# Whole gate or up matrices as buffer units in a decoder layer's expert stage, and a second entry buffer

## The chip, the core and the metric

The kernel runs on one core of one Trainium2 chip. The metric is the device time of one execution in microseconds (us), as the median of several runs. Five engines with queues of their own work side by side: TensorE (PE, matrix products; its weight loads are shown as PEld), VectorE (DVE), ScalarE (ACT), GpSimd (POOL) and SyncE (SP), which here issues all loads of weights. Sixteen DMA engines carry the bytes out of the chip's main memory. Order between engines is kept by semaphores that the kernel counts by hand.

## The reference

One decoder layer over 256 tokens of width 2048, float32. The change touches its last block only, the mixture of experts: 32 experts of inner width 256 in 4 groups; each token goes to two experts of one group.

```python
combine = jnp.sum(jax.nn.one_hot(flat, N_EXPERTS) * wts[..., None], axis=1)   # two weights per token
for grp in range(N_GROUPS):
    sl = slice(grp * EXPERTS_PER_GROUP, (grp + 1) * EXPERTS_PER_GROUP)
    hid = (jax.nn.silu(jnp.einsum("nd,edf->nef", hf, w_gate[sl]))
           * jnp.einsum("nd,edf->nef", hf, w_up[sl]))
    y = y + jnp.einsum("nef,efd->nd", hid * combine[:, sl, None], w_down[sl])
x = x + y;  out = rmsnorm(x, lnf_g)
```

Each expert has three matrices of 2 MiB: gate and up (2048 x 256), down (256 x 2048).

## The kernel before, in words

Experts are worked on in 16 pairs (`NPAIR`). Tokens are first sorted by expert with products against one-hot matrices (`gather`, line 1554), which fill `hs`, all entries by expert in 16 chunks of 128 model columns. For each pair the entries of its two experts (64 places each, `CAP`) are copied out of `hs` into one buffer, `hs_pair`: by ACT and DVE for pair 0 (`gathered`, lines 2145 and 2792), by POOL for the others (`copied_pair`, line 3063). POOL waits before each half of the copy until the pair before has done with these chunks.

On PE a pair runs through these steps:

- gate and up (`gate_up`, line 1593, in four quarters of four chunks): per chunk and expert one product of the 64 entries with 512 columns, gate's 256 and up's 256 together. The two experts use two halves of the array and of the PSUM bank. A float32 product is recorded as two passes.
- after tanh (ACT), `hidden_1` and `hidden_2` (DVE): `hidden_transposes`, and a copy by ACT
- down (`down`, line 1638): four quarters of 512 columns; ACT casts each to a high part, DVE forms the low part (`osp`, two buffers)
- scatter (`scatter`, line 1676): eight products that bring the results to token order; DVE adds each to `x` (line 2837), which frees its bank
- `pair_slots` (line 1574): transposes of the pair's one-hot matrices and its weights, in banks that the scatter uses too

The steps of successive pairs are interleaved in an order written out by hand (lines 1687 to 1753).

The weights come through eight buffers of 2 MiB (`units_at`). A gate and up unit holds half of the chunks of both matrices, gate and up side by side (`gate_up_unit`, line 282), and is filled by two DMAs of 1 MiB; a down unit holds a whole matrix. `unit_of` (line 290) numbers the units in the order of loading, the buffer is the number modulo 8. SP issues a load when the unit's former reader is done (`unit_free`, line 811). For the first three units that reuse a buffer this is done by chunks (`chunk_half_free`, line 825, eight DMAs of 512 KiB per pair of units), for the last pairs by quarters (`last_gate_up_free`, `last_down_free`).

Of the kernel before, what the change touches and what calls it, by code (L numbers as in the profile page):

```python
# [77 lines left out]
def decoder_layer(nc, x_in, mem, ln1_g, w_in, cmp_pos_k, cmp_w1_k, cmp_w2_k, cmp_pos_v, cmp_w1_v,  # L78
# [5 lines left out]
    with ctx:  # L84
# [181 lines left out]
        late_square_junk = over("late_square_junk", entries_end, 2, NT, 512, dtype=mybir.dt.bfloat16)  # L266
        osp = [take_over(f"down_hi_lo_{i}", 2, 512) for i in range(2)]
# [14 lines left out]
        def gate_up_unit(i):  # L282

            return expert_unit[i].rearrange("p (g c n) -> p g c n", g=2, n=FF)
# [13 lines left out]
        def halves_done(p, half):  # L298

            return 2 * half + p + 1 if p < 2 else 2 * p + half + 1  # L300

        down_units = {unit_of(p, 2, e) for p in range(NPAIR) for e in range(2)}

        def filled(u):

            return sum(64 if NSLOT <= v < NSLOT + 6 else 16 if v in down_units else 32
                       for v in range(u % NSLOT, u + 1, NSLOT))
# [267 lines left out]
        pe_first_gu = sem("moe_first_gate_up_quarters")  # L575
        last_gate_up = [[sem(f"last_gate_up{k}_quarter{q}_full") for q in range(2)] for k in range(2)]
# [118 lines left out]
        def _(sp):  # L695
# [64 lines left out]
            def load_unit(expert, kind, i, full):  # L760

                if kind < 2:
                    for gu, src in enumerate((moe_w_gate, moe_w_up)):
                        w = src[0, bass.ds(expert, 1)].rearrange("e (p c) n -> p (e c) n", p=P)
                        sp.dma_start(gate_up_unit(i)[:, gu], w[:, kind * (NC // 2):kind * (NC // 2) + NC // 2, :])\
                            .then_inc(full, 16)
                else:
                    w = moe_w_down[0, bass.ds(expert, 1)].rearrange("e (p c) n -> p (e c) n", p=P)
                    sp.dma_start(down_unit(i), w).then_inc(full, 16)
# [41 lines left out]
            def unit_free(p, kind, e):  # L811

                before = unit_of(p, kind, e) - NSLOT
                for q in range(NPAIR):
                    for k in range(3):
                        if before in (unit_of(q, k, 0), unit_of(q, k, 1)):
                            sp.wait_ge(*((pe_dq, 4 * q + 4) if k == 2 else (pe_gu, halves_done(q, k))))
# [7 lines left out]
            def chunk_half_free(p, kind, k):  # L825

                for half in range(2):
                    if half == 0:
                        sp.wait_ge(pe_first_gu, k)
                    for e in range(2):  # L830
                        u = unit_of(p, kind, e)
                        i = u % NSLOT
                        if half:
                            unit_free(p, kind, e)
                        for f in range(2):
                            if kind < 2:
                                c = NC // 4 * half
                                w = (moe_w_gate, moe_w_up)[f][0, 2 * p + e].rearrange("(p c) n -> p c n", p=P)
                                dst, src = gate_up_unit(i)[:, f, c:c + NC // 4], w[:, kind * (NC // 2) + c:kind * (NC // 2) + c + NC // 4, :]
                            else:  # L840
                                cs = slice(half * (D // 2), half * (D // 2) + D // 2)
                                w = moe_w_down[0, 2 * p + e].rearrange("(p c) n -> p c n", p=P)
                                dst, src = down_unit(i)[:, f, cs], w[:, f, cs]
                            sp.dma_start(dst, src).then_inc(unit_full[i], 16)
# [2288 lines left out]
```

## Time and profile before

| | us |
|---|---|
| median of 3 runs | 1442.5 (1440.79 to 1442.7) |
| profiled execution, its own time | 1443.8 |
| its span | 1442.0 |
| PE busy | 1385.3 (96%) |
| DVE busy | 733.4 (51%) |
| ACT busy | 508.3 (35%) |
| POOL busy | 139.6 (10%) |

The granted TensorE clock is 0.992 of full speed over the span. The expert stage begins at about 962 us and takes the last third. The span runs from the first to the last instruction; times in the views count from its start. Busy time of PE includes time in which a started product waits in the pipeline; the chain of waits and the DMA rows tell more of what sets the end.

### The profile page before, as it was taken

What the parts mean: (1) busy time and instruction counts of PE and PEld (TensorE: products, weight loads), DVE (VectorE), ACT (ScalarE), POOL (GpSimd) and SP (SyncE); (2) the same over time, 40 slices, a digit from 0 to 9 for tenths busy, and PEclk for the clock granted to TensorE, in tenths of its full rate; (3) what the DMA queues carried; (4) which work ended last, traced back from release to release, by engine and by line L of the source; (5) the groups of instructions that cost most, each with busy time, mean ns of one, the idle gap of its engine ahead of it and who ended that gap; (6) DMA issues with size and microseconds to landing.
All of it is one profiled execution on the core that took longest, in us unless ns stands there. A gap on an engine that the chain in (4) does not pass through costs nothing.

```text
span 1442.0 us, 27027 instructions
## 1 busy us (share of the span) xinstructions
PE 1385.3 (96%) x11565; PEld 1041.5 (72%) x11565; DVE 733.4 (51%) x1297; ACT 508.3 (35%) x880; POOL 139.6 (10%) x335
## 2 busy tenths in 40 slices
PE   7999999999999999999999999999999999889996
PEld 7998989888899998887889988874343333334332
DVE  4684947667567556545554443653332332223326
ACT  5553434334265455555454344422111100101003
POOL 8010010201200000000000000012011111011100
PEclk9999999999999999999999999999999999999999
DMA  7633332333395544537537517588999999999997
GB/s 223 211 118 119 126 118 82 106 126 119 119 311 161 174 137 158 175 117 273 193 120 231 175 59 233 185 350 319 420 423 423 424 424 422 422 423 426 422 407 261
DMA packets 150575, 350.99 MB, mean 243 GB/s; under 512 B 13536, under 2 KB 95034, under 8 KB 131898
## 3 DMA queue, kind: packets, MB, share of 16 engines
q1 hardware_dynamic: 150458, 349.30, 65.3%
q8 instruction: 89, 1.46, 0.4%
q14 instruction: 28, 0.23, 0.0%
HBM read 347.18 MB, written 2.10 MB: 242 GB/s over the span
## 4 chain that ended last, share of the span: by engine, by line
PE 87%; DMA 6%; DVE 4%; issue 2%; ACT 1%; POOL 0%; SPq 0%; DVEq 0%; POOLq 0%; ACTq 0%
PE banks L981 22%; PE banks L1589 13%; PE banks L1389 12%; PE banks L1630 6%; PE banks L937 6%; DMA expert_unit<-in_moe_w_down_dram 6%; PE banks L1454 5%; PE banks L1672 4%; PE banks L976 2%; PE banks L1478 1%; PE banks L1501 1%; PE banks L1161 1%; PE banks L1438 1%; PE banks L1400 1%; PE banks L1188 1%
## 5 line engine op out<-in xcount | busy, mean ns | idle before, releaser
L981 PE MATMUL banks<-hidden_lo_chunks,piece 128*128 128x256 f32 x920 | 259.8, 282 | 0.0
L1589 PE MATMUL banks<-expert_unit,pair_entries 128*64 128x512 f32 x1024 | 240.1, 613 | 18.9 <-issue 18.2
L1857 ACT CAST piece<-arena_fixed 128x1024 fp32r<-128x1024 f32 (+1 forms) x158 | 161.4, 1031 | 172.1 <-PE banks L981 136.3
L2304 DVE TENSOR_TENSOR piece<-arena_fixed,piece 128x1024 fp32r<-128x1024 f32 (+1 forms) x158 | 187.8, 1214 | 39.1 <-ACT piece L1857 38.6
L1589 PEld LDWEIGHTS banks<-expert_unit,pair_entries 128*64 128x64 f32 x1024 | 72.4, 140 | 156.5 <-issue 154.1
L981 PE MATMUL banks<-hidden_hi_high_chunks,piece 128*128 128x256 f32 x928 | 178.2, 290 | 1.5 <-DVE hidden_lo_chunks L2287 1.5
L981 PE MATMUL banks<-hidden_hi_low_chunks,piece 128*128 128x256 f32 x912 | 176.2, 291 | 0.0
L981 PEld LDWEIGHTS banks<-hidden_lo_chunks,piece 128*128 128x128 f32 x920 | 175.7, 191 | 0.0
L2568 DVE TENSOR_TENSOR loop_split<-arena_fixed,loop_split 128x2048 fp32r<-128x2048 f32 x48 | 107.9, 2288 | 101.6 <-ACT loop_split L2035 101.6
L981 PEld LDWEIGHTS banks<-hidden_hi_high_chunks,piece 128*128 128x128 f32 x928 | 144.1, 191 | 6.4 <-issue 2.2
L2835 DVE TENSOR_TENSOR arena_phases<-arena_phases,banks 128x512 f32<-128x512 f32 x128 | 81.8, 681 | 131.1 <-PE banks L1672 131.1
L981 PEld LDWEIGHTS banks<-hidden_hi_low_chunks,piece 128*128 128x128 f32 x912 | 141.6, 191 | 6.5 <-issue 3.7
L1389 PE MATMUL banks<-loop_split,act_over_concat 128*128 128x512 f32 x384 | 128.7, 390 | 0.0
L2035 ACT CAST loop_split<-arena_fixed 128x2048 fp32r<-128x2048 f32 x48 | 89.6, 1921 | 83.5 <-PE banks L1389 74.5
L2166 ACT CAST down_hi_lo<-banks 128x512 fp32r<-128x512 f32 x64 | 37.5, 587 | 227.4 <-PE banks L1672 129.9
L1630 PE MATMUL banks<-expert_unit,hidden_turned 128*64 128x512 f32 x512 | 114.0, 594 | 1.4 <-DMA expert_unit<-in_moe_w_down_dram 1.4
L2827 DVE TENSOR_TENSOR down_hi_lo<-banks,down_hi_lo 128x512 fp32r<-128x512 f32 x64 | 44.2, 690 | 100.6 <-ACT down_hi_lo L2166 100.6
L1630 PEld LDWEIGHTS banks<-expert_unit,hidden_turned 128*64 128x64 f32 x512 | 37.5, 137 | 71.9 <-issue 71.4
L1389 PE MATMUL banks<-loop_split,act_over_hT 128*128 128x512 f32 x256 | 89.2, 389 | 0.0
L1389 PEld LDWEIGHTS banks<-loop_split,act_over_concat 128*128 128x128 f32 x384 | 72.1, 188 | 15.0
L3071 POOL COPY pair_entries<-entries_by_expert 128x256 f32 (+1 forms) x124 | 43.8, 398 | 324.1 <-PE banks L1589 324.0
L1672 PEld LDWEIGHTS banks<-down_hi_lo,scatter_onehots 128*128 128x128 f32 x256 | 45.3, 188 | 37.6 <-issue 27.8
(431 smaller groups left out, 2006.3 us busy)
## 6 DMA issues: line engine op xcount, KB each, us to landing
expert_unit<-in_moe_w_gate_dram SPq DMA_DIRECT2D x56, 1024.0 KB, 22.1
expert_unit<-in_moe_w_up_dram SPq DMA_DIRECT2D x56, 1024.0 KB, 24.9
expert_unit<-in_moe_w_down_dram SPq DMA_DIRECT2D x26, 2048.0 KB, 24.2
arena_fixed<-in_w_in_dram SPq DMA_DIRECT2D x22, 2048.0 KB, 8.9
arena_fixed<-in_wk_mem_dram SPq DMA_DIRECT2D x8, 2048.0 KB, 8.9
arena_fixed<-in_wv_mem_dram SPq DMA_DIRECT2D x8, 2048.0 KB, 8.4
arena_fixed<-in_w_out_dram SPq DMA_DIRECT2D x8, 2048.0 KB, 7.9
arena_fixed<-in_wq_mem_dram SPq DMA_DIRECT2D x8, 2048.0 KB, 8.6
```

Source lines behind the costliest of these rows:

```text
L937: mm = pe.matmul(bank[tt][:, :], hidden_x(x_, c)[:, tt * P:tt * P + P], piece_half(p, w_)[:, c2, :], start=c + t == 0, stop=c == NC - 1 an ...
L981: mm = pe.matmul(b[:, half * T:half * T + T], w(w_)[:, k % 8, :], hidden_x(x_, c), start=c + t == 0 and n > 0, stop=c == NC - 1 and t == 2 ...
L1389: mm = pe.matmul(b, src(x_, cc)[:, half * P:half * P + P], lspl[2 * s + h][:, y_, c * WC:c * WC + WC], start=s + h + c + k == 0, stop=end)
L1454: mm = pe.matmul(b, lspl[2 * s + h][:, y_, at:at + P], src(x_, NC // 2 * h + c), start=h + c + k == 0, stop=h == 1 and c == NC // 2 - 1 an ...
L1589: mm = pe.matmul(bank[b][o, :].rearrange("p (g n) -> p g n", g=2), hs_pair[:, c, o], gate_up_unit(i(e))[:, :, c % (NC // 2), :], start=c = ...
L1630: mm = pe.matmul(bank[4 + q][o, :], tTs[:, turn, f, o], down_unit(i(e))[:, f, q * 512:q * 512 + 512], start=f == 0, stop=f == 1)
L1672: mm = pe.matmul(bank[b][:, :], Gt[:, turn, f % 2, :], osp[q % 2][:, half, :], start=half == 0, stop=half == 1)
L1857: nc.scalar.copy(piece_half(p, 0), raw_piece(p)).then_inc(piece_hi, 1)
L2035: nc.scalar.copy(lspl[2 * s + h][:, 0, :], slot(s)[:, h * HU:h * HU + HU]).then_inc(loop_hi, 1)
L2304: V.tensor_tensor(piece_half(p, 1), raw_piece(p), piece_half(p, 0).bitcast(F32), ALU.subtract)\
L2568: V.tensor_tensor(sl[:, 1, :], slot(s)[:, r:r + HU], sl[:, 0, :].bitcast(F32), ALU.subtract)\
L2835: return TT(xs, xs, bank[b][:, :], ALU.add)
```

## The change: what it does

A unit of gate and up is now one whole matrix, gate or up, in one DMA of 2 MiB. A pair's products run through all 16 chunks of gate (256 columns each) and then through all of up, in halves of eight chunks; `gate_up(p, kind, half)` replaces `gate_up(p, quarter)`. Pair 1's entries go to a buffer of their own, `second_entries`, in the memory in which `osp` lies later; so POOL copies them without waiting for pair 0, and all of pair 1's gate and up precedes pair 0's down. The order on PE in the first pairs changes accordingly, and so does the order of ACT (casts of pair 0 before pair 1's tanh) and DVE. The first three units that reuse a buffer are loaded by halves of 1 MiB in another order, the last pair's by halves too. POOL's copies of later pairs wait for the up half instead of the gate and up half.

```diff
+        second_entries = over("second_pair_entries", r5.at, NC, P, dtype=F32)
...
-            return expert_unit[i].rearrange("p (g c n) -> p g c n", g=2, n=FF)
+            return expert_unit[i].rearrange("p (c n) -> p c n", n=FF)
...
-            return 2 * half + p + 1 if p < 2 else 2 * p + half + 1
+        first_order = ((0, 0, 0), (0, 1, 0), (1, 0, 0), (0, 0, 1), (0, 1, 1), (1, 0, 1), (1, 1, 0), (1, 1, 1))
+        def halves_done(p, kind, half):
+            return first_order.index((p, kind, half)) + 1 if p < 2 else 4 * p + 2 * kind + half + 1
...
+                w = (moe_w_gate, moe_w_up, moe_w_down)[kind][0, bass.ds(expert, 1)]
+                sp.dma_start((down_unit if kind == 2 else gate_up_unit)(i),
+                             w.rearrange("e (p c) n -> p (e c) n", p=P)).then_inc(full, 16)
...
+            def half_free(p, kind, half, reader):
+                sp.wait_ge(pe_gu, halves_done(*reader, half))
+                rows = NC if kind < 2 else FF // P
+                cs = slice(half * rows // 2, half * rows // 2 + rows // 2)
+                for e in range(2):
+                    i = unit_of(p, kind, e) % NSLOT
+                    w = (moe_w_gate, moe_w_up, moe_w_down)[kind][0, 2 * p + e].rearrange("(p c) n -> p c n", p=P)
+                    sp.dma_start((down_unit if kind == 2 else gate_up_unit)(i)[:, cs], w[:, cs]).then_inc(unit_full[i], 16)
...
-            chunk_half_free(1, 1, 1)
-            chunk_half_free(1, 2, 2)
-            chunk_half_free(2, 0, 3)
+            for half in range(2):
+                half_free(1, 1, half, (0, 0))
+                half_free(2, 0, half, (0, 1))
+                half_free(1, 2, half, (1, 0))
...
-            def gate_up_chunk(b, c, i):
+            def gate_up_chunk(b, c, kind, i, entries=hs_pair):
                 for e in range(2):
                     o = slice(e * CAP, e * CAP + CAP)
-                    mm = pe.matmul(bank[b][o, :].rearrange("p (g n) -> p g n", g=2), hs_pair[:, c, o],
-                                   gate_up_unit(i(e))[:, :, c % (NC // 2), :], start=c == 0, stop=c == NC - 1)
+                    mm = pe.matmul(bank[b][o, kind * FF:kind * FF + FF], entries[:, c, o], gate_up_unit(i(e))[:, c, :],
+                                   start=kind == 0 and c == 0, stop=kind == 1 and c == NC - 1)
...
+                if p == NPAIR - 1:
+                    pe.wait_ge(last_gate_up[kind][half], 32)
+                elif half == 0 or p < 2:
+                    for e in range(2):
+                        pe.wait_ge(unit_full[place(e)], filled(unit_of(p, kind, e)))
+                if p and kind == 0:
+                    pe.wait_ge(pool_pair, 2 * p + half - 1)
+                for c in range(half * NC // 2, half * NC // 2 + NC // 2):
+                    if p == 0 and kind == 0 and c % 4 == 0:
+                        pe.wait_ge(act_pair, c // 4 + 1)
...
-            gate_up(0, 0)
-            gate_up(0, 1)
+            gate_up(0, 0, 0)
+            gate_up(0, 1, 0)
             gather(8)
             gather(9)
-            gate_up(1, 0)
-            gate_up(1, 1)
+            gate_up(1, 0, 0)
             for c in range(10, NC):
                 gather(c)
-            gate_up(0, 2)
+            gate_up(0, 0, 1)
             pair_slots(0)
-            gate_up(0, 3)
+            gate_up(0, 1, 1)
+            gate_up(1, 0, 1)
             pair_slots(1)
-            gate_up(1, 2)
             hidden_transposes(0)
-            gate_up(1, 3)
+            gate_up(1, 1, 0)
+            gate_up(1, 1, 1)
             down(0)
-            scatter(0, 0)
-            scatter(0, 1)
             for p in range(2, NPAIR - 1):
-                gate_up(p, 0)
+                gate_up(p, 0, 0)
                 if p == 2:
-                    scatter(0, 2)
-                    scatter(0, 3)
+                    for q in range(4):
+                        scatter(0, q)
+                    pair_slots(2)
+                    gate_up(2, 0, 1)
+                    hidden_transposes(1)
                 else:
                     pair_slots(p)
-                hidden_transposes(p - 1)
-                gate_up(p, 1)
-                if p == 2:
-                    pair_slots(2)
+                    hidden_transposes(p - 1)
+                    gate_up(p, 0, 1)
                 down(p - 1)
...
-                if 1 < p < NPAIR - 1:
+                if 0 < p < NPAIR - 1:
                     for q in range(4):
                         down(p - 1, q)
                 act.wait_ge(dve_gt, p + 1)
-                act.wait_ge(pe_gu, halves_done(p, 1))
+                act.wait_ge(pe_gu, halves_done(p, 1, 1))
                 tanh(p % 2).then_inc(act_th, 1)
-                if p == 1:
-                    for q in range(4):
-                        down(0, q)
...
-                            ins = G_.tensor_copy(hs_pair[:, c0:c1, at:at + SEG],
+                            ins = G_.tensor_copy((second_entries if p == 1 else hs_pair)[:, c0:c1, at:at + SEG],
...
-                    pool.wait_ge(pe_gu, halves_done(p - 1, half))
+                    else:
+                        pool.wait_ge(pe_gu, halves_done(0 if p == 2 else p - 1, 1, half))
```

## Rows read from the trace of the kernel before

**Rows 1.** The page's slices, 36 us each: GB/s of the core's DMA.

```profile
GB/s 223 211 118 119 126 118 82 106 126 119 119 311 161 174 137 158 175 117 273 193 120 231 175 59 233 185 350 319 420 423 423 424 424 422 422 423 426 422 407 261
```

**Rows 2.** Windows: stretch; its length; busy time per engine; clock; DMA share; GB/s.

```profile
1060.00:1350.00 290.00, 272.93 (x1212) 107.87 (x1208) 91.99 (x181) 31.94 (x60) 42.25 (x120) 0.98 1.01 423
...
971.00:979.00 8.00, 7.51 (x46) 4.39 (x46) 6.59 (x31) 4.22 (x13) 2.71 (x8) 1.00 0.02 8
979.00:981.00 2.00, 2.00 (x12) 0.59 (x10) 1.31 (x10) 0.00 (x0) 0.00 (x0) 1.00 0.58 129
981.00:990.00 9.00, 8.29 (x44) 3.70 (x42) 0.75 (x1) 0.69 (x1) 1.43 (x4) 1.00 0.99 364
990.00:1010.00 20.00, 20.00 (x108) 9.12 (x106) 5.46 (x21) 4.10 (x13) 6.12 (x20) 1.00 1.03 411
```

**Rows 3.** Chain of waits in the expert stage: start us, length us, what.

```profile
1081.91 6.87 PE banks L1630 x32
...
1108.13 6.87 PE banks L1630 x32
...
1349.83 2.69 issue
1352.52 5.35 PE banks L1589 x16
```

**Rows 4.** Window in which the last weights arrive.

```profile
1422.00:1426.00 4.00, 4.00 (x19) 1.67 (x16) 1.93 (x4) 1.07 (x2) 0.00 (x0) 1.00 0.65 264
```

**Rows 5.** Timeline, the last down quarter: start us, us, engine, line, operation.

```profile
1426.52 1.94 PE L1630 MATMUL banks<-expert_unit,hidden_turned 128*64 128x512 f32 x8
```

**Rows 6.** Timeline, SP's issues: first reuse, pair 3's first unit, pair 2's down.

```profile
978.65 0.33 SPq L844 DMA_DIRECT2D expert_unit<-in_moe_w_gate_dram  x1
...
1010.29 0.33 SPq L765 DMA_DIRECT2D expert_unit<-in_moe_w_gate_dram  x1
...
1028.68 0.80 SPq L769 DMA_DIRECT2D expert_unit<-in_moe_w_down_dram  x2
```

**Rows 7.** DMA view: packets in 978:1010, in 1014:1031 and in 1033:1040.

```profile
DMA packets 3214, 11.76 MB, mean 367 GB/s; under 512 B 349, under 2 KB 349, under 8 KB 3211
...
DMA packets 988, 7.18 MB, mean 423 GB/s; under 512 B 112, under 2 KB 112, under 8 KB 112
...
DMA packets 203, 3.01 MB, mean 431 GB/s; under 512 B 19, under 2 KB 19, under 8 KB 19
```

**Rows 8.** Chain of waits, pairs 0 and 1.

```profile
982.66 1.10 POOL pair_entries L3071 x3
...
990.98 3.06 PE banks L1560 x24
994.05 3.58 PE banks L1589 x16
...
998.34 3.58 PE banks L1589 x16
...
1010.25 6.87 PE banks L1630 x32
...
1036.37 3.43 PE banks L1589 x16
```

**Rows 9.** Timeline after pair 0's down: scatter and DVE's adds.

```profile
1017.04 2.13 PE L1672 MATMUL banks<-down_hi_lo,scatter_onehots 128*128 128x512 f32 x8
...
1021.36 0.68 DVE L2835 TENSOR_TENSOR arena_phases<-arena_phases,banks 128x512 f32<-128x512 f32 x1
...
1023.46 2.48 DVE L2835 TENSOR_TENSOR arena_phases<-arena_phases,banks 128x512 f32<-128x512 f32 x4 [1.43 <-PE banks L1672]
```

**Rows 10.** Groups of instructions by shape (busy us, mean ns); last, a timeline row.

```profile
L1589 PEld LDWEIGHTS banks<-expert_unit,pair_entries 128*64 128x64 f32 x890 | 63.0, 141 | 140.1 <-issue 138.1 <-DMA expert_unit<-in_moe_w_up_dram 0.3
...
L1501 PE MATMUL banks<-arena_phases 128*128 128x256 f32 x64 | 14.4, 381 | 0.8 <-ACT arena_phases L2116 0.8
...
955.67 1.06 PE L1520 MATMUL banks<-arena_fixed,arena_phases 128*36 128x256 f32 x8 [0.23 <-DVE arena_fixed L2279]
```

More of the change, by code:

```diff
@@ L574, in decoder_layer @@
         pe_gu, pe_dq = sem("moe_gate_up_half"), sem("moe_down_quarter")
-        pe_first_gu = sem("moe_first_gate_up_quarters")
-        last_gate_up = [[sem(f"last_gate_up{k}_quarter{q}_full") for q in range(2)] for k in range(2)]
+        last_gate_up = [[sem(f"last_{k}_half{h}_full") for h in range(2)] for k in ("gate", "up")]
         last_down = [[sem(f"last_down{k}_quarter{q}_full") for q in range(4)] for k in range(2)]
@@ L823, in pair_free @@
                     load_expert(p, kind, e)
[L825 to L844, printed above, removed]
@@ L882, in _ @@
             load_expert(0, 2, 1)
-            chunk_half_free(1, 1, 1)
-            chunk_half_free(1, 2, 2)
-            chunk_half_free(2, 0, 3)
+            for half in range(2):
+                half_free(1, 1, half, (0, 0))
+                half_free(2, 0, half, (0, 1))
+                half_free(1, 2, half, (1, 0))
             pair_free(3, 0)
@@ L1603, in gate_up @@
                     for e in range(2):
-                        pe.wait_ge(unit_full[place(e)], filled(unit_of(p, half, e)))
-                if p == 0:
-                    pe.wait_ge(act_pair, q + 1)
-                    if q:
-                        pe.wait_ge(dve_pair, q)
-                elif p == 1:
-                    pe.wait_ge(pool_pair, max(q, 1))
-                elif q % 2 == 0:
-                    pe.wait_ge(pool_pair, 2 * p + half)
-                for c in range(4 * q, 4 * q + 4):
-                    mm = gate_up_chunk(p % 2, c, place)
@@ L1620, in hidden_turned @@
+                mm.then_inc(pe_gu, 1)
             def hidden_turned(b):
@@ L1734, in _ @@
             before, last = NPAIR - 2, NPAIR - 1
-            gate_up(last, 0)
+            gate_up(last, 0, 0)
             pair_slots(last)
             hidden_transposes(before)
-            for q in range(1, 4):
-                gate_up(last, q)
+            gate_up(last, 0, 1)
+            gate_up(last, 1, 0)
+            gate_up(last, 1, 1)
             late_down(before, 0)
@@ L1761, in _ @@
                         slots(0, lambda tt: round_weights[:, tt, :], 1, 0, 1, 2 * P).then_inc(over_gt, 1)
[L1762 removed]
+                        pe.wait_ge(over_full, v * 96 + 96)
                         pe.wait_ge(over_copied, v + 1)
[L1764 to L1765 removed]
+                        for kind in range(2):
+                            for c in range(NC):
+                                mm = gate_up_chunk(0, c, kind, lambda e: 2 * kind + e + 1)
                         mm.then_inc(over_gu, 1)
@@ L2859, in outputs @@
                     add(p, f)
-            pair_slots(0)
-            pair_slots(1)
-            hidden(0)
-            hidden(1)
-            outputs(0)
-            for p in range(2, NPAIR):
+            for p in range(NPAIR):
                 pair_slots(p)
-                if p < NPAIR - 1:
+                if 0 < p < NPAIR - 1:
                     outputs(p - 1)
@@ L3076, in copied_pair @@
                     c0 = NC // 2 * half
-                    if p == 1 and half:
-                        pool.wait_ge(act_hs, 3 * NC // 8)
-                        pool.wait_ge(dve_hs, 3 * NC // 8)
-                        pool.wait_ge(pe_first_gu, 3)
-                        copied(c0, c0 + NC // 4)
-                        c0 += NC // 4
                     if p == 1:
```

53 lines of the change are left out of this document (16 added, 37 removed).

## The prediction

> **What bounds the kernel now.** I read the page's slices first: in 29 to 39 of the 40 the DMA engines move 407 to 426 GB/s without a pause, in 26 to 28 they are at 185 to 350 [rows 1]. That is the expert stage: 32 experts of three 2 MiB matrices, 201 MB. The windows say the same over 290 us: 423 GB/s at a DMA share of 1.01 [rows 2]. One pair of experts is 12.58 MB, so 12.58 / 0.423 = 29.7 us of DMA. PE's work for a pair is the distance of two successive down products in the chain, 1108.13 - 1081.91 = 26.2 us [rows 3]. So between about 1130 and 1352 PE waits once or more per pair. The last long wait is the 2.69 us before 1352.52, ahead of pair 13's second gate and up unit; after it the chain is PE to the end, 76 us [rows 3]. The DMA engines empty at about 1424.6 (0.65 of the window from 1422) and the last down quarter starts at 1426.52 [rows 4, 5], so the two finish 2 us apart. The end is therefore the time at which the weights arrive, plus a PE tail that has almost no room in it. What must be followed is the DMA queue: when it starts, when it is empty, and how fast it runs.
>
> It is empty once: from 971 to 979 it moves 8 GB/s [rows 2]. All eight buffers are full then, and the first is free only when pair 0's first group of matmuls is done; SyncE (SP) issues at 978.65 [rows 6]. From then on it is fed, just: at 1010.29 pair 3's first unit is issued when the bytes ahead of it are nearly gone (below).
>
> **Packets.** This is the term with the sign. The same stage holds transfers cut three ways. From 978 to 1010, halves of half-matrices in 512 KB transfers: 3214 packets, 349 of them tiny, the others 11.76 / 2865 = 4.1 KB, and 411 GB/s once they flow, in 990 to 1010 [rows 2, 7]. From 1014 to 1031, half-matrices in 1 MB transfers: 988 packets, 112 of them tiny, the others 8.2 KB, 423 GB/s. From 1033 to 1040, whole down matrices in one 2 MB transfer: 203 packets, 19 of them tiny, the others 16.4 KB, 431 GB/s [rows 7]. The change loads whole gate and up matrices in one transfer of 2 MB, 16 KB contiguous per partition on both sides, like down; its half loads have 8 KB rows where they had 4 KB.
> Units that change from 8 to 16 KB after the queue's tightest point: pair 3's up, and gate and up of pairs 4 to 13, 21 units of 4.19 MB up to the one that ends the last wait, 88.1 MB. At 423 they take 208.3 us, at 431 204.4: 3.9 us less. The 423 over 290 us [rows 2] is a mixture, a third of it down; if down runs at 431, the rest runs at 419 (1/423 = (1/3)/431 + (2/3)/419), and the gain is 210.3 - 204.4 = 5.9. Bounds: 0, if the rate is a property of down, and 5.9. I take 4.5, between the two ways of reading it.
> Here the page "DMA: Bandwidth & Descriptors" of the Trainium skill (Rules for kernel authors) speaks against the change: it asks for 128 partitions and at least 1 MiB per DMA for maximum bandwidth, and both forms have that. The rows differ, 423 against 431; by the page this term would be 0 (rival a).
>
> **The start.** Pair 0's first release is unchanged: before, four chunks in eight passes of 512 columns (gate and up together, two passes a chunk, the two experts side by side); now eight chunks of gate alone in 16 passes of 256. By 990 the queue has moved 0.26 + 3.28 = 3.5 MB of the six first half loads (12.58 MB) [rows 2]; the other 9.05 MB take 22.0 us at 411 and 21.4 at 423, so they end at 1011.4, not 1012.0. Pair 3's first and pair 2's second unit (8.39 MB) follow until 1030.9 (431) in place of 1031.9 (423). Both gains count only if the next transfer is there by then: pair 2's down.
>
> **The order on PE up to pair 0's down.** The same products in another order: before, both early halves of pair 1 stand ahead of the last gathers, now one does. The wait for POOL's copy between 982.66 and 983.8 goes [rows 8], because pair 1 has its own buffer and POOL's copies need the gathers alone: 0.7 us. The six half loads are released after the groups of pairs 0 and 1, at 978.6, 982.1, 986.8, 993.5, 997.8 and 1001.2 (groups of 3.58, last gathers 3.06, slots 998.34 - 997.63 = 0.71 [rows 8]); before, the fourth came at 991. 2.1 MB take 5.0 us, so the queue still holds. One new wait: pair 1's up needs all of its unit, and its second half is the fourth load. Bytes up to it: 8.39 MB, at 990 + 4.9/0.423 = 1001.6; how long after its last byte a load is seen, no row shows, and PE is there at 1002.3. I charge 0.3 us (0 to 1.5). Behind it on PE stand pair 0's down and all that follows. So pair 0's down starts at 1010.25 - 0.7 + 0.3 = 1009.9 [rows 8], and pair 3's gate is issued at 1009.9 instead of 1010.29: in time for 1011.4.
>
> **Pair 2, where the change costs.** Pair 1's tanh now comes after ScalarE's (ACT's) four casts of pair 0's down, pair 0's four scatters stand together behind pair 2's first gate half, then slots 2, the second gate half, pair 1's transposes, pair 1's down. Before, two scatters came before that group and two after it, and slots stood later, so VectorE (DVE) kept up. In the timeline the scatter starts at 1017.04; DVE ends its fourth add 5.0 us after (1022.04), and the other four take 2.48 [rows 9]. All adds of pair 0 (which slots 2 waits for, since the banks are shared) are thus done 7.5 us after the first scatter; PE has 4.1 us of scatters to fill it. Now: down 1009.9 + 6.87 = 1016.8, gate half 3.43 -> 1020.2, +7.5 -> 1027.7, slots 0.71, second gate half 3.58 -> 1032.0. That is the release of pair 2's down (it takes the buffers of pair 2's gate), 3.3 us later than the 1028.68 of before [rows 6]. Bytes flow about 1.0 us after an issue (issue 978.65, then 0.58 of the two us from 979 [rows 2, 6]), so at 1033.0, where the queue is empty from 1030.9 on and before had them flow at 1031.9. Cost 1.1 us; but the 16 engines run empty one by one, not at once, so I charge 0.7 (0 to 2.5; 2.5 if PE comes another 1.5 late). The start's gain is spent in this. After pair 1's transposes no matmul covers ACT's copy any more (0.6 us of PE); PE is then 3.5 us late, but later releases are ahead of the queue: pair 3's up is issued at about 1040, while pair 2's down flows until 1042.7. PE has 29.7 - 26.2 = 3.5 us to make up per pair and does, before 1352.
>
> **The matmuls.** 256 columns instead of 512, and twice as many weight loads. The two experts' products run side by side: 16 records, 8 passes of 512 columns, in 3.43 us [rows 8], 0.43 per pass. The nearest rows with 256 columns: the memory values, 64 in 14.4 us, so 0.225 each with the starts of the groups, against half of 0.43 = 0.215; and the router's logits, two tiles of 36 columns side by side, 4 times two in 1.06 us with start and end, at most 0.265 [rows 10]. In the tail from 1352.5 the ten groups left hold 160 new passes: at 0.225 1.6 us, at 0.265 8.0, at 0.215 nothing; I take 0.3, since both rows hold starts and ends that a long run does not have. While PE waits for weights it costs nothing.
> A weight load is 141 ns long [rows 10] and fits under 215, and weight loads of two tiles stand under 256 columns in the logits' row. The page "TensorE: Matmul & The Clock Gate" of the Trainium skill (Part 3: Packing small matmuls) lets weight loads overlap running matmuls only in other row groups, and all rows are in use here; its section LDWEIGHTS gives 64 / 1.2 = 53 ns, which then would show in every pass (rival b). With 512 columns nothing of a load shows in 0.43 per pass [rows 8], so the trace so far is against the page; no row has tiles of 64 columns with 256.
>
> **At the end** the last pair's gate and up come in the same 2.1 MB steps, 8 KB rows for 4 KB (0.6 us earlier, not needed by PE). Copies for the next pair start later (after the up half), with a scatter and a group of 3.58 still ahead of their use: nothing.
>
> **Sum** against the profiled execution (span 1442.0, its own time 1443.8): -4.5 + 0.7 + 0.3 = -3.5, and -0.4 for the last wait, shorter now: the group after it took 5.35 us in place of 3.58 [rows 3, 8], and may not (1.8, at a chance of a fifth). -3.9: 1439.9 for that execution, which stood 1.3 over the median 1442.5 of the runs; so 1438.6.
>
> **Rivals.** (a) The change doesn't do what it says: 16 KB gives nothing for gate and up. For: down differs in more than its packets. Against: three sizes, three rates in order. 1442.5 + 0.7 + 0.3 - 0.4 = 1443.1. (b) Slower: weight loads no longer hide under 256 columns. Place: the 160 passes of the tail, which nothing can overtake. It decides, to 0.2% slower, from (3.9 + 2.9) / 160 = 42 ns left over per pass; half of the 141 gives 160 x 0.07 = 11.2, so 1449.8. Against: 0.225 at 128-column loads that are longer. By the page's 53 ns it would be 8.5, so 1447.1. (c) The stall at pair 2 is dearer: 2.5 in place of 0.7, 1440.4. For: three idle times of PE in a row there. Against: the queue empties bit by bit. (d) The slow group after the last wait goes, 1.4 more than counted, and the weights behind it are early enough: 1437.2. For: the wait was 2.69 and each pair's DMA is now shorter. Against: the queue is at its limit up to the end.
>
> **Chances.** Forecast 0.56 (1437.4 to 1440.2), (a) 0.14, (b) 0.10, (c) 0.08, (d) 0.12. The range leaves out (b) and the far side of (d): 1436.0 to 1443.8. A measurement tells 0.2%, 2.9 us: faster is below 1439.6. That holds 0.42 of the forecast, (d), and 0.01 of (c): 0.55; slower, over 1445.4, is (b): 0.10; same 0.35.
>
> **What would show it.** Packets of 16 KB at 431 GB/s in stretches of gate and up; the gate and up products at 0.215 to 0.22 per pass; a hole in the DMA row near 1031 to 1033; PE idle twice before slots 2; POOL's wait at 983 gone; the chain's last DMA wait near 1349. Wrong, if gate and up stay at 423, if the hole is over 3 us, or if PE has no DMA wait after 1100.

## The result, and the profile after

The changed kernel takes 1444.8 us (median of 20 runs, 1441.1 to 1447.1), the kernel before 1442.4 beside it: ratio 1.0015, 95% interval 1.0009 to 1.0021. Forecast were 1438.6 and a range of 1436.0 to 1443.8. The change makes the kernel slower, by 2.2 us after the ratio (2.4 by the two medians), where 3.9 us less were expected. That is clear of the noise, though less than the 0.2% that the prediction took for what a measurement tells. The profiled execution took 1447.0 (span 1445.3), 2.2 over the median; that matters below.

The windows of the changed kernel (stretch, length, busy time of PE, its weight loads, DVE, ACT and POOL, clock, DMA share, GB/s): the steady stage, the end of the weights, then two us at a time behind pair 0's down.

```profile
1060.00:1350.00 290.00, 276.41 (x1884) 158.43 (x1882) 92.58 (x182) 33.07 (x62) 43.31 (x124) 0.98 1.01 427
...
1422.00:1426.00 4.00, 4.00 (x18) 1.64 (x18) 2.59 (x5) 0.86 (x2) 0.00 (x0) 1.00 0.72 287
...
1026.00:1028.00 2.00, 0.77 (x5) 0.81 (x5) 1.89 (x4) 0.00 (x0) 0.00 (x0) 0.77 1.07 459
1028.00:1030.00 2.00, 2.00 (x11) 1.42 (x13) 0.71 (x4) 0.00 (x0) 0.00 (x0) 0.50 0.99 426
1030.00:1032.00 2.00, 2.00 (x14) 1.05 (x12) 0.00 (x0) 0.00 (x0) 0.00 (x0) 0.50 0.54 221
1032.00:1034.00 2.00, 2.00 (x14) 1.14 (x12) 0.00 (x0) 0.00 (x0) 0.00 (x0) 0.53 0.06 25
1034.00:1036.00 2.00, 1.54 (x12) 0.79 (x10) 0.00 (x0) 0.37 (x1) 0.00 (x0) 1.00 0.40 74
1036.00:1038.00 2.00, 2.00 (x12) 0.68 (x10) 0.00 (x0) 0.31 (x1) 0.00 (x0) 1.00 0.72 262
```

The steady rate is 427 GB/s instead of 423 [rows 2], at the same share of busy DMA: the sign of the packets' term is right. But from 1030 to 1038 there is a hole in a queue that was full before, 2.3 MB or 5 us deep, and TensorE's clock is granted at half, its level of 1.2 GHz, from about 1027 to 1034, ahead of the hole and into it.

The chain of waits of the same execution (start, length, what), pairs 0 to 2 and the last wait:

```profile
982.27 3.60 PE banks L1571 x32
985.87 3.06 PE banks L1542 x24
...
992.95 9.23 DMA expert_unit<-in_moe_w_up_dram
...
1002.32 7.13 PE banks L1571 x64
1009.45 6.87 PE banks L1605 x32
1016.32 3.45 PE banks L1571 x32
...
1024.09 3.00 DVE arena_phases L2808 x5
...
1028.53 6.27 PE banks L1571 x32
...
1352.79 31.74 DMA expert_unit<-in_moe_w_up_dram
...
1384.67 7.13 PE banks L1571 x64
```

POOL's wait [rows 8] is gone: the gather at 981.12 is followed by pair 1's gate at once. The 16 passes of 256 columns take 3.45 to 3.60 us, as the 8 of 512 did. Pair 1's up waits for its second half load: 9.23 us from issue to landing, for the last 0.98 of which PE is idle. Behind pair 2's first gate half, PE waits for DVE's adds, and the second gate half takes 6.27 us instead of 3.60. The longest of these waits stands ahead of slots 2 (PE's timeline; in brackets the idle time and what ended it):

```profile
1027.23 0.66 PE L1550 MATMUL banks<-arena_fixed,slot_onehots 128*128 128x128 f32 x2 [1.89 <-DVE arena_phases L2808]
```

SP's issues, pair 3's gate and pair 2's down, stand at 1009.48 and 1034.85, where they were at 1010.29 and 1028.68 [rows 6]. Counted from the first gather product, which this execution reaches at 968.77 and the kernel before at 969.95, they come 0.4 and 7.3 us later than before:

```profile
1009.48 0.80 SPq L762 DMA_DIRECT2D expert_unit<-in_moe_w_gate_dram  x2
...
1034.85 0.80 SPq L762 DMA_DIRECT2D expert_unit<-in_moe_w_down_dram  x2
```

**Where the time went.** The executions reach the first gather product at anything from 967.0 to 970.7 us (two of one program, the split kernel, 2.9 us apart), so spans are compared behind that point. The trace has the semaphore events of each unit's landing; cut at landings, the expert stage of every profiled execution reads as follows (us; "up" is from the first gather to the landing of pair 2's up, "down" from there to pair 2's down, "next" to pair 3's up, "steady" to pair 14's up, "end" to the last instruction). The last two columns, taken up below, count the fetches of TensorE's instructions over the DMA engines: first those in "steady" and the 12 us ahead of it, then those in "end".

```
kernel                        up     down   next   steady   end    sum     fetches
before                       63.74   9.81   9.96   328.64  59.90  472.04   11  3
before, again                64.05   9.79   9.94   328.20  59.59  471.57   11  3
before, 256 columns          64.17   9.79   9.93   329.44  61.27  474.61   17  4
changed                      64.99  13.59  11.13   326.04  60.75  476.51   18  4
changed, again               65.12  10.25  10.98   326.28  60.35  472.98   18  4
changed, PE kept busy        64.78  12.27   9.63   326.32  60.17  473.16   18  4
changed, wide products       64.66  10.33  10.77   324.76  59.95  470.47   12  3
changed, two loads           64.49  13.09  10.98   329.54  60.70  478.79   18  4
split scatters               63.74   9.79   9.84   326.06  60.71  470.14   18  4
split scatters, again        64.82   9.79   9.79   326.31  61.10  471.80   18  4
split, slots later           63.91   9.77  12.26   326.02  60.89  472.86   18  4
split, wide products         64.06   9.79   9.78   324.89  59.48  468.00   12  3
```

Against the kernel before (mean of two) the profiled execution of the changed one has +1.1 at the start, +5.0 at pair 2 ("down" and "next" together, 24.72 against 19.75), -2.4 in the steady stretch and +1.0 at the end.

### The profile page after: what moved, and what is told of

It reads as the page before. It is cut to its first block, busy times and chain, and to the rows that moved or that the text cites. A ratio compares the mean times of both kernels' runs of the same rounds, so it can differ in the third digit from the quotient of the medians.

```text
span 1445.3 us, 28994 instructions
## 1 busy us (share of the span) xinstructions
PE 1387.5 (96%) x12589; PEld 1121.9 (78%) x12589; DVE 734.0 (51%) x1297; ACT 507.8 (35%) x880; POOL 138.7 (10%) x331
## 4 chain that ended last, share of the span: by engine, by line
PE 83%; DMA 10%; DVE 4%; ACT 1%; issue 1%; SPq 0%; DVEq 0%; ACTq 0%
PE banks L963 22%; PE banks L1571 12%; PE banks L1371 12%; DMA expert_unit<-in_moe_w_up_dram 9%; PE banks L919 6%; PE banks L1605 6%; PE banks L1436 5%; PE banks L1647 3%; PE banks L958 2%; PE banks L1460 1%; PE banks L1483 1%; PE banks L1143 1%; PE banks L1420 1%; PE banks L1382 1%; PE banks L1170 1%
## 5 line engine op out<-in xcount | busy, mean ns | idle before, releaser
L1571 PE MATMUL banks<-expert_unit,pair_entries 128*64 128x256 f32 x1920 | 227.0, 391 | 13.9 <-DMA expert_unit<-in_moe_w_up_dram 13.9
L1833 ACT CAST piece<-arena_fixed 128x1024 fp32r<-128x1024 f32 (+1 forms) x158 | 161.4, 1031 | 171.8 <-PE banks L963 134.6
L1571 PEld LDWEIGHTS banks<-expert_unit,pair_entries 128*64 128x64 f32 x1920 | 142.3, 140 | 95.1 <-issue 36.2
L1647 PE MATMUL banks<-down_hi_lo,scatter_onehots 128*128 128x512 f32 x256 | 69.6, 411 | 1.3 <-DVE down_hi_lo L2800 1.3
L3039 POOL COPY pair_entries<-entries_by_expert 128x256 f32 x112 | 40.3, 402 | 304.4 <-PE banks L1571 304.4
```

Of the source, the lines that this page charges most:

```text
L1571: mm = pe.matmul(bank[b][o, kind * FF:kind * FF + FF], entries[:, c, o], gate_up_unit(i(e))[:, c, :], start=kind == 0 and c == 0, stop=kin ...
L1647: mm = pe.matmul(bank[b][:, :], Gt[:, turn, f % 2, :], osp[q % 2][:, half, :], start=half == 0, stop=half == 1)
L1833: nc.scalar.copy(piece_half(p, 0), raw_piece(p)).then_inc(piece_hi, 1)
```

## The experiments

Ratios are to the kernel before, with 95% intervals.

**1. Split scatters.** From the changed kernel, one order on PE:

```diff
                 if p == 2:
-                    for q in range(4):
-                        scatter(0, q)
-                    pair_slots(2)
-                    gate_up(2, 0, 1)
-                    hidden_transposes(1)
+                    scatter(0, 0)
+                    scatter(0, 1)
+                    gate_up(2, 0, 1)
+                    scatter(0, 2)
+                    scatter(0, 3)
+                    pair_slots(2)
+                    hidden_transposes(1)
```

> The changed kernel with pair 2's second gate half moved from behind all four scatters of pair 0 to between the second and the third of them (one order on TensorE, nothing else). Theory (the handover): pair 2's down transfers were issued at 1034.85 because the second gate half stood behind two gaps of TensorE (1021.4 to 1022.4, 1024.95 to 1027.2) and then ran at a granted clock of 0.5. With the half ahead of the second gap I expect the issue at 1024 to 1027, the granted clock near 1 in that half (about 3.6 us in the chain instead of 6.27), no stretch under 300 GB/s between 1030 and 1036, pair 2's down landed near 1044 instead of 1047.4, and 3 to 4 us less than the changed kernel: a ratio to the kernel before of 0.9985 to 0.9995 (about 1440.8 us). Rival (the hole is made up later, since the ring of eight units evens it out, or the time is made elsewhere): ratio stays at 1.0015, 1444.8 us, with the hole gone or not.

Measured: 1441.3 us, 0.9996 (0.9987 to 1.0005). The windows and SP's issue:

```profile
1028.00:1030.00 2.00, 1.54 (x10) 0.51 (x10) 0.41 (x4) 0.37 (x1) 0.00 (x0) 1.00 0.98 418
1030.00:1032.00 2.00, 2.00 (x12) 0.70 (x10) 0.69 (x1) 0.59 (x1) 0.00 (x0) 1.00 0.98 418
1032.00:1034.00 2.00, 2.00 (x12) 0.72 (x10) 0.69 (x1) 0.59 (x1) 0.00 (x0) 1.00 1.07 459
```

```profile
1023.63 0.81 SPq L762 DMA_DIRECT2D expert_unit<-in_moe_w_down_dram  x2
```

Counted from the first gather product, the issue comes 10.2 us earlier than in the changed kernel; the hole is gone, and its time is not made up elsewhere: the rival falls.

**2. The same again.**

> The kernel with the split scatters once more, beside the one with the later slot products. Theory (handover): ratio 0.9991 to 0.9999, as the 0.9996 of its first rounds, and in the profile no stretch under 300 GB/s between pair 2's up and its down, with 9.8 us between their landings. Rival (the first rounds were lucky, and the hole comes back in some executions): ratio above 1.0003.

Measured: 1442.9 us, 1.0005 (0.9996 to 1.0014). The ratio missed the expected range; the handover did not: 9.79 us between the landings again, no hole. Between the two profiles the first gather product differs by 2.9 us and "up" by 1.1 (64.82 against 63.74); what differs between the runs without a profile is not shown. Both sets together put this kernel level with the kernel before, 2 us below the changed one (ratios 0.9996 and 1.0005 against 1.0015 and 1.0015).

**3. The changed kernel again.**

> The changed kernel itself once more, beside the others on the same chip. Theory (the clock decides in each execution): ratio 1.0010 to 1.0018 as before with a spread of 5 us or so, and in this profile either a granted clock of 0.5 in pair 2's second gate half with 13 us or more from the landing of pair 2's up to that of its down, or a clock of 1 and 10 to 11 us; nothing between. Rival (the handover always costs the same): 13 us whatever the clock was.

Measured: 1444.2 us, 1.0015 (1.0004 to 1.0025). In this profile the clock did not fall:

```profile
1026.00:1028.00 2.00, 0.12 (x2) 0.06 (x1) 2.00 (x5) 0.00 (x0) 0.00 (x0) 1.00 1.02 434
1028.00:1030.00 2.00, 2.00 (x18) 1.55 (x20) 1.35 (x6) 0.00 (x0) 0.00 (x0) 1.00 0.99 426
1030.00:1032.00 2.00, 2.00 (x22) 1.29 (x18) 0.00 (x0) 0.00 (x0) 0.00 (x0) 1.00 0.90 377
1032.00:1034.00 2.00, 1.54 (x10) 0.66 (x8) 0.00 (x0) 0.37 (x1) 0.00 (x0) 1.00 0.69 164
1034.00:1036.00 2.00, 2.00 (x12) 0.71 (x10) 0.16 (x1) 0.58 (x1) 0.00 (x0) 1.00 0.80 319
```

```profile
1027.98 0.41 PE L1550 MATMUL banks<-arena_fixed,slot_onehots 128*128 128x128 f32 x2 [1.88 <-DVE arena_phases L2808]
```

```profile
1032.37 0.80 SPq L762 DMA_DIRECT2D expert_unit<-in_moe_w_down_dram  x2
```

The same waits, but the second gate half takes 3.6 us and the release stands at 1032.4. The hole is 2 us deep instead of 5 (860 KB missing from 1030 to 1036 at 430 GB/s), and "down" and "next" cost 21.23 us, 1.5 more than before. So the handover is dear at either clock: 1.5 us without the fall, 5.0 with it. Two more profiles of this order agree: 21.10 us with the clock held (wide products), 24.07 with a fall (two loads).

**4. PE kept busy.** Between the fourth scatter and slots 2 of the changed kernel, six products whose result nobody reads:

```diff
                         scatter(0, q)
+                    pe.wait_ge(dve_sc, 3)
+                    for i in range(6):
+                        pe.matmul(bank[4][:, 0:T], hs[:, 0, 0:P], hs[:, 0, 0:T], start=True, stop=True)
                     pair_slots(2)
```

> The changed kernel with TensorE's second gap at pair 2 filled: behind the fourth scatter of pair 0 it does six products of 256 columns whose result nobody reads (about 0.43 us each by the chain's 3.45 us for 16 passes of half that), and the order stays. Theory (the granted clock): in the profiled run of the changed kernel pair 2's second gate half ran at a granted clock of 0.5 after two gaps (6.27 us instead of 3.60), which let the release of pair 2's down slip from about 1032 to 1034.85 and made a hole of 3.8 us; where the clock did not fall (the profile of the kernel with wide products, same order) the hole was 0.5 us. With the gap filled I expect a granted clock near 1 from 1026 to 1034, pair 2's down landed 10.0 to 10.6 us after its up instead of 13.6, and 2 to 3 us less than the changed kernel: ratio 0.9995 to 1.0003. Rival (the stall itself, not the clock, makes the hole): 13 us or more between the two landings, ratio 1.0012 to 1.0018.

Measured: 1444.0 us, 1.0014 (1.0005 to 1.0022): a miss. The clock is 1.00 throughout and the release at 1032.04, yet the median stays. "Down" and "next" are 21.90 us: the products filled the wait and ran over its end, so that slots 2 start 59.0 us after the first gather instead of 58.5, and the hole remains.

```profile
1025.09 2.75 PE L1693 MATMUL banks<-entries_by_expert 128*128 128x256 f32 x12
```

```profile
1030.00:1032.00 2.00, 2.00 (x21) 1.11 (x17) 0.00 (x0) 0.00 (x0) 0.00 (x0) 1.00 0.62 262
1032.00:1034.00 2.00, 1.54 (x9) 0.73 (x10) 0.00 (x0) 0.37 (x1) 0.00 (x0) 1.00 0.66 147
```

The theory that the clock decides in each execution falls: with the clock held the hole is still 2.2 us deep in time and the median has not moved. The clock explains 3.5 us of the one execution that the comparison began with. That the order sets the loss is shown by experiments 1 and 2. A share of the falls in the median is not excluded: the products delay the release by 0.5 us themselves, and the intervals, about 1.2 us to either side, could hide 1 us.

**5. Two loads.** The changed kernel with each whole gate or up matrix in two DMAs of 8 chunks, so 8 KB from each row in place of 16:

```diff
+                    for half in range(2):
+                        cs = slice(half * NC // 2, half * NC // 2 + NC // 2)
+                        sp.dma_start(gate_up_unit(i)[:, cs], w[:, cs]).then_inc(full, 16)
```

> The changed kernel with each whole gate or up matrix loaded by two DMAs of 1 MB (8 chunks each, 8 KB from each row) where it has one of 2 MB (16 KB); waits and releases as they are. Theory of the prediction (longer packets carry faster): two units land every 9.8 us for 16 KB packets and I expect 9.9 to 9.95 us here, so that the 21 units from pair 4 to pair 14 and the 22 or so of gate and up bring 4 to 5 us more: 1449 us, ratio 1.0045 to 1.005. Rival (the faster landings do not come from the length of the packet): ratio 1.0010 to 1.0020, as the changed kernel, and the landings of full units keep 4.89 us each. The fetches of instructions should be as many as in the changed kernel (24 of 16 KB from 960 to 1430) under both.

Measured: 1448.3 us (5 runs), 1.0039 (1.0026 to 1.0052), 3.5 us over the changed kernel. Its steady window:

```profile
1060.00:1350.00 290.00, 275.19 (x1866) 158.41 (x1864) 91.59 (x181) 32.54 (x61) 42.61 (x121) 0.98 1.01 423
```

423 GB/s is the rate of before, and the steady stretch is 329.54 us against 326.0 to 326.3, with PE's stream as in the changed kernel. The packets' term is real and 3.4 us large (forecast 4.5). Half units land 2.48 us apart and whole ones 4.90: 0.07 us for each of the 44 gate and up units in the stretch. Both forms have 128 partitions and 1 MiB or more per DMA; by the rule of the Trainium skill's page "DMA: Bandwidth & Descriptors" (Rules for kernel authors) they would be equal, and here the measurement decides against it. The edit halves the row and doubles the number of DMAs at once, and no run here separates these two. For DMAs of one size, 512 KB, the rate does differ with the row: 411 GB/s with 4 KB rows [rows 2], 387 with the 2 KB rows that make up most of the last down loads (the kernel before, 1410 to 1420).

**6. Wide products.** The changed kernel from pair 3 on with one product of 512 columns for two chunks, by the first chunk's entries; the second chunk's own entries are left out, so this is a probe of the shorter stream and not a version of the layer:

```diff
+                    if p >= 3:
+                        if c % 2 == 0:
+                            for e in range(2):
+                                o = slice(e * CAP, e * CAP + CAP)
+                                mm = pe.matmul(bank[p % 2][o, :], hs_pair[:, c, o], flat(gate_up_unit(place(e))[:, c:c + 2, :]),
+                                               start=kind == 0 and c == 0, stop=kind == 1 and c == NC - 2)
```

> The changed kernel with TensorE's products of gate and up from pair 3 on taken two chunks at once: one product of 512 columns with the first chunk's entries as weights in place of two of 256 with their own. The columns that pass, the releases and the transfers stay; the second chunk of each two is so multiplied with the wrong entries (the output is not the reference's), and TensorE's stream is shorter by 104 instructions or so for every pair, as in the kernel before. Theory (instruction fetches): the jumps of about 1.45 us in the landings at 1053.6, 1197.1 and 1360.0 of the changed kernel come from every eighth fetch of TensorE's instructions (24 of 16 KB from 960 to 1430, 16 in the kernel before). I expect 17 or 18 fetches here, one such jump or none where there were three, the stretch from pair 2's down to pair 14's first gate unit 334 to 335.5 us long instead of 337.1, and 2 to 3 us less than the changed kernel: ratio 0.9995 to 1.0003. Rival (the jumps belong to the 16 KB packets or to DRAM): the jumps stay at their places, ratio 1.0012 to 1.0020.

Measured: 1442.6 us, 1.0007 (0.9998 to 1.0015), about 1.2 us below the changed kernel after the ratios, with intervals that overlap. Fetches of instructions from 960 to 1430, in the DMA view (queue, kind, packets, MB, share), one fence each for the changed kernel, the kernel before and the wide products of experiment 7:

```profile
q8 instruction: 24, 0.39, 0.3%
```

```profile
q8 instruction: 16, 0.26, 0.2%
```

```profile
q8 instruction: 19, 0.31, 0.3%
```

That queue q8 is TensorE's is read from its count, which follows the length of TensorE's stream. In the changed kernel's trace each of these 16 KB packets takes 0.93 to 1.27 us of a DMA engine's time, 1.06 on average. Units land 4.85 to 4.94 us apart, but for three steps of 6.2 to 6.4 that end at 1053.6, 1197.1 and 1360.0. The fetches just ahead of these start at 1048.1, 1193.2 and 1357.4, and each is the eighth after the one before. In the wide kernel the large steps (5.9 and 6.4 us) end at 1048.6 and 1275.4, 227 us apart instead of 143 and 163, and again the fetches just ahead of them (1043.0 and 1272.8) are eight apart. The kernel before has no step of that size, but eight of 5.1 to 5.4 us, each within 7 us behind a fetch. "Steady" is 324.76 instead of 326.0 to 326.3.

**7. Wide products without the hole:** experiments 1 and 6 together.

> The kernel with the split scatters (pair 2's second gate half between them) and also with the products of gate and up from pair 3 on taken two chunks at once, 512 columns by the first chunk's entries: the second chunk of each two is multiplied with the wrong entries (the output is not the reference's), columns, releases and transfers stay, TensorE has about half as many instructions in them. There is no hole at pair 2 to blur the comparison. Theory (instruction fetches): 18 or 19 fetches of 16 KB from 960 to 1430 instead of 25, the jumps of 1.0 to 1.5 us in the landings every 225 us or so instead of every 158, one round of them instead of two between pair 2's down and pair 14's first unit, that stretch 334 to 334.5 us long instead of 335.9, and 1 to 1.6 us less than with the split scatters alone (1441.3): ratio 0.9984 to 0.9990. Rival (the jumps are DRAM's or the queue's own): two rounds of jumps at the same spacing, ratio 0.9993 to 1.0000.

Measured: 1439.6 us, 0.9984 (0.9975 to 0.9992), 1.7 and 3.0 us below the two sets of the split kernel after the ratios. "Steady" 324.89, "end" 59.48; with the split scatters alone 326.06 and 326.31, 60.71 and 61.10. The landings are late once by 1.2 us (at 1244.0) and three times by 0.2 to 0.3, where the split kernel had two pairs of 1.0 and 0.4. So PE's longer stream costs 1.3 us in the steady stretch and 1.2 to 1.6 at the end. The 15 fetches of the changed kernel in 1060 to 1350 are 0.25 MB, 0.6 us of 427 GB/s, and the 10 here 0.4 us of it: the bytes alone are not it.

Most of the loss at the end stands behind the last weights, in the stores of the output (issues, KB each, us to landing: the split kernel, the wide one, the kernel before):

```profile
out_dram<-arena_phases SPq DMA_DIRECT2D x1, 256.0 KB, 3.3
```

```profile
out_dram<-arena_phases SPq DMA_DIRECT2D x3, 256.0 KB, 2.2
```

```profile
out_dram<-arena_phases SPq DMA_DIRECT2D x8, 256.0 KB, 2.2
```

In all seven profiles of the changed and split kernels with their narrow products a fetch starts within 0.9 us behind the first store's issue (1437.5 behind 1436.9 in the changed kernel), and it is 7.9 to 8.5 us from that issue to the end. In the other five the last fetch starts 2.7 us or more ahead of that issue, and it is 7.3. So this part, 0.6 to 1.2 us, hangs on where a fetch happens to fall; no edit tested it by itself.

**8. Narrow products in the kernel before**, from pair 3 on: the matmul part of the change alone.

```diff
+                        for g in range(2):
+                            for e in range(2):
+                                o = slice(e * CAP, e * CAP + CAP)
+                                mm = pe.matmul(bank[p % 2][o, g * FF:g * FF + FF], hs_pair[:, c, o],
+                                               gate_up_unit(place(e))[:, g, c % (NC // 2), :],
+                                               start=c + g == 0, stop=c == NC - 1 and g == 1)
```

> The kernel before with each product of 512 columns of gate and up from pair 3 on taken as two of 256 (gate, then up): the matmul part of the change alone, with the loads, buffers and order of before. Theory (instruction fetches): 22 or 23 fetches of 16 KB from 960 to 1430 instead of 16, and the stretch between the landings of pair 2's down and of pair 14's first unit grows from 338.6 us by 2 to 3: ratio 1.0014 to 1.0020, about 1445 us. Rival (weights and columns alone matter, and 256 columns cost what 512 do per column, 3.45 us for 16 passes): ratio 0.9997 to 1.0003. Second rival (weight loads not hidden under 256 columns, as my prediction's slower case had it): the last group of 16 products grows by 1 us or more and the time by 4 to 8.

Measured: 1443.1 us, 1.0007 (0.9998 to 1.0016): too small to be told from nothing by the runs. The profile has the same sign: 23 fetches for 16, "steady" +1.0 and "end" +1.5 on the mean of the two profiles of before. The +1.5 is not the fetches' doing, as far as the profile shows: PE reaches pair 14's up 1.8 us after its landing, where it was 0.6 and 0.1 in the two profiles of before, because one group behind the last wait (1350.7) took 6.57 us at the lower clock, and the stores take no longer than before. Rival (b) of the forecast (weight loads not hidden) would have made 4 to 8.

**9. Slots later.** The split kernel with pair 1's slot products behind its up:

```diff
-            pair_slots(1)
             hidden_transposes(0)
             gate_up(1, 1, 0)
             gate_up(1, 1, 1)
+            pair_slots(1)
```

> The kernel with the split scatters, and pair 1's slot products (0.7 us in the chain: 0.37 and 0.34) moved from before pair 1's up to behind it. Pair 3's gate transfers are issued when pair 1's up is done (39.8 us after the first gather in the split kernel), and the DMA shows a dip from 40 to 44 us after that gather (352 and 381 GB/s of 430). Theory (the start is held by TensorE's own work between releases): the issue comes 0.7 us earlier, the dip shrinks, pair 2's up lands 0.3 to 0.6 us earlier than 63.7 us after the first gather, and 0.3 to 0.6 us less than the split kernel. Rival (GpSimd's one-hots and copies for pair 2, which begin behind these slot products and took 5.5 us, now come late for pair 2's gate, or the dip stays): no gain, or 0.5 us or so lost; TensorE waits before pair 2's first gate half.

Measured: 1442.9 us, 1.0009 (1.0001 to 1.0018), no gain. Chain:

```profile
992.43 9.20 DMA expert_unit<-in_moe_w_up_dram
...
1001.76 7.13 PE banks L1571 x64
...
1030.79 8.78 PE banks L1605 x32
```

PE came earlier and only waited longer for the second half load of pair 1's up: 1.54 us, where the two profiles of the split kernel have 0.1 and 0.7. Here it is this load that holds the work at the start, not PE's own. Pair 1's down took 8.78 us in place of 7 (the clock at 0.50 from 1032 to 1034), and "next" is 2.5 us longer.

**10. The kernel before again**, one profile.

> The kernel before once more, for a second profile of it. Both theories: from the first gather to pair 2's up 63.7 us, 9.8 us more to its down, 338.6 us more to pair 14's first gate and up unit, 59.9 us from there to the end, each within about 0.4 us; what lies ahead of the first gather may differ by 2 us between executions, which would be the greater part of the spread of the kernel's runs. If the parts behind the first gather differ by more than 1 us, single profiles are too rough for the terms that I read from them.

1441.7 us; the stretches agree with the first profile within 0.45 us, the time ahead of the first gather is 1.6 us shorter.

## Why the prediction was wrong, step by step

- **Packets: right in kind, smaller in size.** -4.5 was forecast, experiment 5 gives -3.4.
- **Pair 2: the step that failed first.** "Cost 1.1 us; but the 16 engines run empty one by one, not at once, so I charge 0.7 (0 to 2.5; 2.5 if PE comes another 1.5 late)." Counted from the first gather product, the release was forecast at 62.1 us and came at 62.8 where the clock held (experiment 3), at 66.1 where it fell. The hole it makes cost 1.5 us in the first case, twice the charge, and 5.0 in the second, outside the stated 0 to 2.5; of the profiles of the changed kernel's order with the wait left open it fell in two of four (the changed kernel, two loads). The forecast saw PE idle twice ahead of a group that releases a buffer, and gave that group its full-clock 3.58 us. Rival (c) named this place, but with 2.5 us as its dear end. A hole of over 3 us was among the forecast's own signs of being wrong; the first execution had 5.
- **The cost that was not in the sum: PE's instruction stream.** "Twice as many weight loads" was worked out as time on PE, and there it is next to nothing: 3.45 to 3.60 us a group, as before. The Trainium skill's page "TensorE: Matmul & The Clock Gate" (Part 3: Packing small matmuls) has weight loads overlap in other row groups only; this trace does not agree. But the doubled instructions are themselves fetched over the DMA engines, 24 packets of 16 KB for 16. The longer stream costs 1.0 to 1.3 us in the steady stretch (experiments 6 to 8) and 0.4 to 1.6 at the end (experiments 6 and 7). It takes back between two fifths and most of what the packets bring, and the sum had no term for it.
- **The start: a gain of 0.6 to 1 was forecast and spent on pair 2.** It was not there. Pair 2's up landed 64.5 to 65.1 us after the first gather with the order of the change, 63.7 and 64.1 before. The new wait of pair 1's up, charged 0.3, is 0.95 to 0.98 us of idle PE in three profiles of that order (the changed kernel twice, PE kept busy), 0.34 with wide products and none with two loads, and pair 3's gate is issued behind it. The split kernels show 63.7 to 64.8, so part of this varies from run to run.
- **The last wait: -0.4 was forecast.** The slow group behind it is gone, but the wait itself is still there, later than forecast: not near 1349 but ahead of pair 14's up (1384.67, 0.56 us of idle PE). The second profile of the kernel before has its last wait at the same place (1380.46, 0.65 us) and no slow group behind it either, so the 5.35 us that this term was read from belonged to one execution's last wait. With the changed kernel "end" is 0.6 to 1.0 longer, for which the sum had nothing.

The stretches of experiment 3, without the fall of the clock, sum to +1.2 (start) + 1.5 (pair 2) - 2.1 (steady) + 0.6 (end) = +1.2 us against the mean of the two profiles of before; those of the first execution, with it, to +4.7. The runs' +2.2 lies between. Rival (a), at 1443.1, came nearest to the measured time, but by luck: its reason, that 16 KB gives nothing for gate and up, is what experiment 5 refutes. How often the clock falls in the runs without a profile stays open, and so does why it does so in one execution and not in the next. That a fetch delays a landing because one of the 16 engines falls behind is argued from the step at every eighth, not shown.

## What to carry to other kernels

When transfers set the time, list every release that a new order moves, with the group of work that stands ahead of it, and if PE idles before that group, price it at the lower clock too, as a bound (6.2 to 6.3 us for 3.6 here). Count instructions as well as columns: halving the width of products lengthens a stream (24 fetches for 16 here) that is loaded over the same DMA engines as the weights. One DMA with 16 KB rows in place of two with 8 KB rows was worth 1.5% of a stream (4.90 for 4.97 us a unit). No complete version here beats the kernel before: the split scatters bring the change level with it, and the one that is faster (0.9984) gets its short stream by wrong entries.

## What had not been expected of the hardware

- A 16 KB instruction packet takes 1.06 us of one DMA engine on average, where 16 KB at a sixteenth of 427 GB/s would be 0.61; and once in eight such fetches the landings come 1.0 to 1.5 us late, for good.
- Two executions of one program, the split kernel, reach the first gather product 2.9 us apart (967.8 and 970.7), more than most terms of this change.
- After gaps of 0.5, 0.5 and 1.9 us in PE's work the clock was granted at 0.50 for over six us in one execution and at 1.00 in another of the same program.
